# Steps of the woven attention blocks stand one by one on TensorE: in the middle of a weight piece, in front of its last chunk, and behind it

## The reference, cut to what matters

```python
# MLA, and in the same form the memory attention (without mask)
s = einsum('bhqd,bhkd->bhqk', q_nope, k_nope) + einsum('bhqr,bkr->bhqk', q_rope, k_rope)
p = softmax(where(mask, s * scale, -inf))
o = einsum('bhqk,bhkd->bhqd', p, v)
# NSA: three such attentions share one query, and their results are summed with gates
out = g[..., 0:1] * o_cmp + g[..., 1:2] * o_sel + g[..., 2:3] * o_win
```

## Time and profile before

| what | value |
|---|---|
| median of three runs | 2646.47 us (2645.66 to 2646.92) |
| the profiled execution, own time | 2647.24 us |
| its span | 2645.4 us |
| PE busy | 2614.7 us, 99% of the span |
| DVE busy | 1791.5 us, 68% |
| ACT busy | 1270.6 us, 48% |
| PE's share of the chain that ended last | 94% |

### The profile page before, as it was taken

One profiled execution on the slowest core, in us unless ns is written; L12 is line 12 of the kernel. 1 busy time (PEld: TensorE's weight loads), 2 busy tenths in 40 slices (PEclk: granted clock), 3 DMA queues, 4 the chain that ended last, 5 costly groups with the idle time before them and its releaser, 6 DMA issues.

```text
span 2645.4 us, 34673 instructions
## 1 busy us (share of the span) xinstructions
PE 2614.7 (99%) x14268; PEld 2256.2 (85%) x14268; DVE 1791.5 (68%) x2140; ACT 1270.6 (48%) x1689; POOL 13.1 (0%) x26
## 2 busy tenths in 40 slices
PE   8999999999999999999999999999999999999998
PEld 7898888888889888888888888888889898899987
DVE  7876897777666686676665545456676658766765
ACT  6546645443545444444443344445454545545554
POOL 0000000000000000000000000000000000000000
PEclk9999999999999999999999999999999999999999
DMA  9998817888685476477766555565656557654343
GB/s 351 363 359 266 271 44 264 313 286 286 223 274 140 129 270 238 143 277 251 246 215 235 192 191 191 190 203 179 191 171 200 181 184 238 210 180 142 97 160 127
DMA packets 339761, 573.53 MB, mean 217 GB/s; under 512 B 22671, under 2 KB 100807, under 8 KB 338328
## 3 DMA queue, kind: packets, MB, share of 16 engines
q1 hardware_dynamic: 336802, 560.45, 63.4%
q0 software_dynamic: 2368, 10.77, 1.2%
q10 hardware_dynamic: 438, 0.15, 0.0%
HBM read 567.11 MB, written 4.21 MB: 216 GB/s over the span
## 4 chain that ended last, share of the span: by engine, by line
PE 94%; DVE 2%; ACT 1%; DMA 1%; issue 1%; SPq 0%; ACTq 0%; DVEq 0%
PE tile_ps L1052 86%; PE misc_ps L1052 6%; DVE w_lo L2251 1%; DMA w_raw<-in_w_in 1%; PE misc_ps L1447 1%; PE misc_ps L1287 1%; DMA w_raw<-in_w_mem_kv 0%; ACT w_hi L1701 0%; DVE probs_t L2362 0%; PE misc_ps L1551 0%; PE misc_ps L1184 0%; ACT mem_t L1942 0%; DVE o_lo L2564 0%; DVE o_hi L2563 0%; DVE var L2561 0%
## 5 line engine op out<-in xcount | busy, mean ns | idle before, releaser
L2251 DVE TENSOR_TENSOR w_lo<-w_raw,w_hi 128x1024 fp32r<-128x1024 f32 x840 | 1012.5, 1223 | 650.9 <-ACT w_hi L1701 646.7
L1701 ACT ACTIVATE w_hi<-w_raw 128x1024 fp32r<-128x1024 f32 x840 | 878.4, 1058 | 1028.3 <-PE tile_ps L1052 958.1
L1052 PE MATMUL tile_ps<-w_hi,h_both 128*128 128x512 f32 x3008 | 818.3, 391 | 1.1 <-DVE h_both L2484 0.8
L1052 PEld LDWEIGHTS tile_ps<-w_hi,h_both 128*128 128x128 f32 x3008 | 561.4, 188 | 119.8 <-issue 5.2
L1052 PE MATMUL tile_ps<-h_both,w_hi 128*128 128x256 f32 (+1 forms) x2624 | 490.9, 312 | 2.1 <-DVE w_lo L2251 1.8
L1052 PE MATMUL tile_ps<-w_lo,h_both 128*128 128x512 f32 x1504 | 464.2, 389 | 0.0
L1052 PEld LDWEIGHTS tile_ps<-h_both,w_hi 128*128 128x128 f32 x2624 | 358.8, 192 | 3.6 <-DVE w_lo L2251 2.4
L1052 PEld LDWEIGHTS tile_ps<-w_lo,h_both 128*128 128x128 f32 x1504 | 282.3, 188 | 59.2
L1052 PE MATMUL tile_ps<-h_both,w_lo 128*128 128x256 f32 x1632 | 289.4, 281 | 0.0
L1052 PEld LDWEIGHTS tile_ps<-h_both,w_lo 128*128 128x128 f32 x1632 | 259.1, 191 | 28.4
L2342 DVE SCALAR_TENSOR_TENSOR probs_t<-w_raw,c_act,probs_t 128x512 f32<-128x512 f32 x210 | 157.7, 751 | 6.6 <-DMA w_raw<-in_ada_w 0.6
(11 more groups left out here) (408 smaller groups left out, 2126.1 us busy)
## 6 DMA issues: line engine op xcount, KB each, us to landing
w_raw<-in_w_in SPq DMA_DIRECT2D x88, 1024.0 KB, 5.2
w_raw<-in_ffn_w_in SPq DMA_DIRECT2D x88, 1024.0 KB, 5.1
w_raw<-in_ada_w SPq DMA_DIRECT2D x64, 1024.0 KB, 5.1
w_raw<-in_w_out SPq DMA_DIRECT2D x48, 1024.0 KB, 5.2
w_raw<-in_ffn_w_down SPq DMA_DIRECT2D x44, 1024.0 KB, 5.2
w_raw<-in_b_w_in SPq DMA_DIRECT2D x33, 1024.0 KB, 5.3
w_raw<-in_ada_w SPq DMA_DIRECT2D x64, 512.0 KB, 6.3
w_raw<-in_a_w_in SPq DMA_DIRECT2D x32, 1024.0 KB, 5.4
```

The lines of the kernel that those rows point to most:

```text
L1052: return nc.tensor.matmul(o, l, r, start=start, stop=stop, skip_group_check=True)
L1701: f(w_hi[CUT_IN.get(s_, s_ % 2)][:, hf], w_raw[r % 4][:, hf], ACT.Copy).then_inc(cut_hi, 1)
L2251: v.tensor_tensor(w_lo[b][:, hf], w_raw[r % 4][:, hf], f32(w_hi[b][:, hf]), ALU.subtract).then_inc(cut_lo, 1)
```

## The change

The last step of an entry stays behind its piece. The steps ahead of it are now called inside the piece: the first in front of its third chunk (number 2 of 0 to 3), that is after half of its matmuls, and of three steps the second in front of the fourth chunk. This is done by a new argument `inside` of `product`, a table from (piece, chunk) to a step. The arithmetic is the same, and so is the order of the steps among themselves. The program order of ACT, DVE, POOL and SP isn't changed at all: listed row by row, those of before and of the changed kernel are the same.

```diff
+        def spread(steps, sizes, piece=0):
+            inside, after, at_ = {}, [], 0
+            for e, n in enumerate(sizes):
+                for k in range(n - 1):
+                    inside[piece + e, 2 + k] = steps[at_ + k]
+                after.append(steps[at_ + n - 1])
+                at_ += n
+            return inside, after
...
-            def product(name, x_hi, x_lo=None, ready=(), chunk_ready=None, between=(), peel=False):
+            def product(name, x_hi, x_lo=None, ready=(), chunk_ready=None, between=(), peel=False, inside={}):
...
                         for c in range(0 if by_halves else g.kc):
                             k = q * g.kc + c
                             begin, end = k == 0, k == g.kp * g.kc - 1
+                            if (e_, c) in inside:
+                                inside[e_, c]()
                             if g.split and c == second:
                                 pe.wait_ge(cut_lo, low + per(i, 2 * g.body * g.kp))
...
-                product(f"mla_qn{hf}", *q_op, ready=done("cq"), between=drain[0:2])
-                product(f"mla_qr{hf}", *q_op, between=drain[2:3])
+                first, second = ({}, {}) if not drain else ({(0, 2): drain[0]}, {(0, 2): drain[3]})
+                product(f"mla_qn{hf}", *q_op, ready=done("cq"), between=drain[1:3], inside=first)
+                product(f"mla_qr{hf}", *q_op, between=drain[4:5], inside=second)
...
-            product("mla_wo", *o, chunk_ready=head_pairs, between=drain + woven[3:])
+            product("mla_wo", *o, chunk_ready=head_pairs, between=[drain[1], drain[2], drain[4]] + woven[3:],
+                    inside={(0, 2): drain[0], (2, 2): drain[3]})
...
+            mem_inside, mem_a = spread(mem_a[2:], MEM_A_GROUPS[1:])
...
+            steps, n = attention_steps("nsa"), [sum(sizes) for sizes in NSA_GROUPS]
+            inside, after = spread(steps[2:n[0]], NSA_GROUPS[0][1:], 5)
+            product("nsa_zq", *h, inside=inside, between=[None] * 4 + [lambda: (nsa_q_ready(), steps[0](), steps[1]())] + after)
+            inside, after = spread(steps[n[0]:], NSA_GROUPS[1])
+            product("nsa_qm", *h, inside=inside, between=after)
+            inside, after = spread(steps[n[0] + n[1]:], NSA_GROUPS[2])
+            product("nsa_zm", *h, inside=inside, between=after)
...
+            inside, after = spread(mem_b[1:], MEM_B_GROUPS[1:], 1)
+            product("nsa_out", *o, chunk_ready=heads_or_mem, inside=inside, between=[lambda: (steps[-1](), mem_b_ready())] + after)
```

More of the change, by code:

```diff
@@ L1495, in _ @@
                 pe.wait_ge(rp_done, ROPE0[f"mla_q{hf}"] + BLK)
-                drain = drained(attention_steps(f"mla{hf}", f"mla_v{hf}"))
+                steps = attention_steps(f"mla{hf}", f"mla_v{hf}")
+                for do in steps[:-5]:
+                    do()
+                drain = steps[-5:]
             fin = lambda a: [(at_fin, FIN0[a] + sum(u["last"] for u in UNITS[a]))]
@@ L1591, in mem_a_ready @@
                 pe.wait_ge(ld_mkv, 32)
-            mem_a = in_groups(attention_steps("mem_a"), MEM_A_GROUPS)
-            product("pool_zm", *h, between=placed({3: lambda: (mem_a_ready(), mem_a[0]())}))
+            mem_a = attention_steps("mem_a")
+            product("pool_zm", *h, between=placed({3: lambda: (mem_a_ready(), mem_a[0](), mem_a[1]())}))
+            mem_inside, mem_a = spread(mem_a[2:], MEM_A_GROUPS[1:])
             def pooled_or_mem(k):
@@ L1602, in _ @@
             product("pool_out", *o, chunk_ready=pooled_or_mem,
-                    between=placed({**{k: do for k, do in enumerate(mem_a[1:])},
+                    inside=mem_inside, between=placed({**{k: do for k, do in enumerate(mem_a)},
                                     **{k: lambda tb=tb: turn_residual("kv", tb) for tb, k in enumerate((9, 11, 14))}}))
@@ L1665, in heads_or_mem @@
                 return [(at_fin, FIN0["nsa"] + k + 2)] if k % 2 == 0 else []
-            product("nsa_out", *o, chunk_ready=heads_or_mem, between=with_mem_b(rest, [mem_b_ready] + mem_b[1:]))
+            inside, after = spread(mem_b[1:], MEM_B_GROUPS[1:], 1)
+            product("nsa_out", *o, chunk_ready=heads_or_mem, inside=inside, between=[lambda: (steps[-1](), mem_b_ready())] + after)
         @block.scalar
```

## The result

| what | before | changed |
|---|---|---|
| median | 2646.69 us (4 runs, 2645.66 to 2647.60) | 2680.32 us (4 runs, 2677.87 to 2683.39) |
| profiled execution | 2647.24 us | 2680.93 us |
| ratio | | 1.0126, 95% interval 1.0114 to 1.0138 |

The change costs 33.6 us, 1.3%. The forecast was 23.8 us and a range that ended at 2677 us: the direction was right, the size was not.

The account below looks back on a forecast made before the run. PE, busy for 99% of the span, bounds the kernel. New waits in NSA 15.9, MLA 5.9 and the last memory attention 2.0 sum to 23.8 us; added to 2646.5 us that gives 2670.3 us, range 2660 to 2677 us.

Parts of the forecast that it names:

- the stock of 5 us: PE's waits for DVE's o_lo (3.5 us) and ACT's transposes copy (1.4 us): about 5 us that spreading could gain.
- the spread gains what it is meant for: Rival: the old sum's write is ready in mid-piece, so only gains are left; 2641 us, chance 0.03.
- The mechanism and the formula: Inner steps whose values open a sum wait for its old write: 2.92 us moved up + 0.14 - slack.
- the sum took 2.0 us off: NSA: ACT starts the next cut 0.2 to 0.9 us sooner at five pieces; estimate 2.0 us, bounds 0 and 4.5.
- the sum has 2.25 us: NSA, the one inner step of `nsa_zq` that opens a sum: slack 0.81 us, so a wait of 2.25 us.
- NSA's 15.9 us: NSA: waits at nine inner steps, 18.9 us, less 1.0 for stalls and 2.0 for ACT's earlier starts.
- MLA's 5.9: MLA: four inner steps that open a sum lose 0.6, 0.8, 2.7 and 1.8 us, 5.9 us in all.
- the last memory attention's 2.0 us: Last memory attention: waits of 1.9 and 2.2 us, less gains of 1.1 and about 1.0 us; together +2.0 us.
- Broken runs at nothing: Breaking runs of weight matmuls at about 30 more places costs nothing; upper bound 0.1 us each, 3 us.
- the clock: Rival: PE's new idles in the attention blocks make the granted clock fall too, 1.7 us a fall; chance 0.10.
- this rival for a few falls: Clock falls behind the three to five new idles above 2.5 us: 5 to 9 us more, 2677 us; chance within 0.10.
- the case with all fifteen falls: Clock falls behind all fifteen new idles: 25 us more, 2696 us; chance 0.02 for nearly all, within the 0.10.

Follow-up runs that it names:

- early write: Changed kernel, but DVE writes each sum at the end of the entry before's last step, ahead of its next weight cut: 2642.28 us, ratio 0.9976.
- filled waits: Changed kernel with matmuls on constants, never read, in all 15 inner steps whose values waited 0.9 us or more for o_lo: 2670.89 us, ratio 1.0086.
- NSA alone: Kernel before the change, with the steps of NSA alone parted as in the change: 2669.57 us, ratio 1.0080.

## Why the prediction was right, and where it was wrong

**What bounds the kernel, and the stock of 5 us: right.** With the early write the spread gains 5.8 us. The stock read from the earlier trace rows was 4.9 us and small stalls; of the 4.9 us, 1.0 is still waited, so some 1.9 us of the gain are stalls too short to be listed as waits. The rival "the spread gains what it is meant for" named 2641 us and its condition, the write ready in the middle of the piece. The early write makes that condition true, and the time is 2642.28 us.

**The mechanism and the formula: right.** The new waits are at the 15 places, ten of them within 0.3 us of the forecast's numbers. One number in the sum was a slip: at the second place of the earlier trace rows the slack of 0.14 us gives 2.92 + 0.14 - 0.14 = 2.92 us, not 3.06; with the 0.39 us that PE waited there already it is 3.31 us. `nsa_qm` and `nsa_zm`, worked out from the earlier trace rows against measured: 2.92 + 0.39 against 3.28, 1.05 against 0.93 and 0.95, 1.94 against 1.85, 2.78 against 2.26, and 2.28 against 1.81 three times. MLA, worked out from the earlier trace rows: 1.6, 2.7, 1.8, 1.8 against 1.39, 2.51, 1.61, 1.71. The last memory attention: 2.2 and 1.9 against 2.12 and 1.59. Four places are half a microsecond shorter, 3 x 0.47 + 0.52 = 1.9 us, and for that the sum took 2.0 us off, for ACT's earlier start of the cut. The two rows of the changed kernel behind the first of these four show it: piece and cut start at

```profile
2478.09 0.72 PE L1062 MATMUL tile_ps<-h_both,w_hi 128*128 128x256 f32 x4
...
2479.19 1.99 ACT L1723 ACTIVATE w_hi<-w_raw 128x1024 fp32r<-128x1024 f32 x2
```

which is 1.10 us apart, where the earlier trace rows has 1.45 us: 0.35 of the 0.47 us. The forecast for PE's waits was over 20 in number and some 25 us; they are 18 and 27.6 us.

**One term was too large.** In `nsa_zq`, at the earlier trace rows's first place, the sum has 2.25 us and the trace 0.95. ACT's cut is why. Before, it began 1.64 us into the piece; these two rows of the kernel before are the start of the piece and the cut:

```profile
2428.83 0.72 PE L1052 MATMUL tile_ps<-h_both,w_hi 128*128 128x256 f32 x4
...
2430.47 1.99 ACT L1701 ACTIVATE w_hi<-w_raw 128x1024 fp32r<-128x1024 f32 x2
```

and these of the changed kernel:

```profile
2435.08 0.72 PE L1062 MATMUL tile_ps<-h_both,w_hi 128*128 128x256 f32 x4
...
2435.52 1.99 ACT L1723 ACTIVATE w_hi<-w_raw 128x1024 fp32r<-128x1024 f32 x2
...
2440.22 0.68 PE L1062 MATMUL misc_ps<-probs_t,v_cmp 15*128 15x128 f32 x4 [0.95 <-DVE o_lo L2586]
```

There it begins 0.44 us into the piece, 1.20 us sooner, because ACT had served the parted step already. The slack that I read from the old trace was itself a product of the grouping. This is the greater part of the 2.0 us by which NSA's 15.9 us differ from the 13.93 us with filled waits. MLA's 5.9 and the last memory attention's 2.0 us measure 5.73 and 2.27 us, and pooling 0.01 us.

**Broken runs at nothing: borne out, not measured.** The version with the early write has all of them and is 5.8 us faster than before; no run prices a break by itself.

**The step that failed: the clock.** The prediction says "by the rows, in which waits below a microsecond do nothing and only one of nearly 3 us did, I keep 2670", gives the rival 0.10, lets "idles above 2.5 us (three to five)" bring a fall, and puts the term at nothing in the sum. The trace of before didn't bear that out. Besides the fall of the earlier trace rows it has one at 154.16 us, which the prediction doesn't mention. In the 4.8 us ahead of it PE waited twice, for 1.18 and for 0.42 us (timeline), and in the last 3.41 us it was busy for 2.98 us (windows):

```profile
150.55 1.95 PE L1052 MATMUL misc_ps<-const,probs_t 128*128 128x1 f32 x16 [1.18 <-DVE probs_t L2362]
152.92 0.74 PE L1052 MATMUL tile_ps<-h_both,w_hi 128*128 128x256 f32 x4 [0.42 <-DVE w_lo L2251]
```

```profile
150.75:154.16 3.41, 2.98 (x26) 2.90 (x26) 2.48 (x4) 1.81 (x2) 0.00 (x0) 1.00 1.05 393
154.16:157.58 3.42, 3.42 (x18) 3.42 (x18) 0.81 (x2) 3.09 (x6) 0.00 (x0) 0.50 1.03 377
```

Behind a wait of 1.38 us at 160.43 the same trace has no fall. So I had put the border near 3 us, where a fall behind much shorter waits already stood against it, and left the whole term out of the sum.

In three profiles of the changed kernel the idles in the attention blocks of 2.12, 2.26 and 3.28 us were followed by a fall each time, that of 2.51 us in two of three, the four of 1.81 to 1.85 us in seven cases of twelve, and none of 1.71 us or less. In the first profile that is eight times 3.41 us at half clock and 12.5 us by the traces, the whole of what was missing: 23.8 us, less 1.9 for terms that were too large, plus 12.5 is 34.4 us, where the table has 34.5. The rule that the prediction weighed, from the Trainium skill, page "TensorE: Matmul & The Clock Gate", section "HAM oscillation — how this bites in real kernels", that PE begins cold after its wait in every turn, held for seven of fifteen waits in the first profile. The forecast of this rival for a few falls, 2677 us, lies 3 us below the median. The chance it was given was too low, and so was the upper end of the range, since the case with all fifteen falls (2696 us) was left outside.

What stays open: what decides whether a fall comes. Idles of 1.84 and 1.85 us in two other kernels, and one of 3.27 us early in a third, had none; the same idle in the same program had one in some executions and not in others. The profiles show that it is neither the program nor the length alone, and no more.

## What to carry to other kernels

Before a step is moved up on one engine, look at what its inputs stand behind in the program order of the others, and move both: here the spread alone cost 34 us, the write ahead of the cut alone gave nothing, and the two together gained 5.8 us (0.24%). When a change makes PE wait where it didn't, price each wait twice, as the wait and as the slower matmuls behind it: here the slower matmuls added 12.5 us to 22.0. Before a term is put at nothing, go through every place of the trace where the effect shows, not the clearest one alone: the trace of before had a fall behind waits of 1.18 and 0.42 us, and it was left out. Where a border isn't known, the range has to hold both sides.

## What the runs showed of the hardware that was not expected

The granted clock fell behind single idles of PE as short as 1.81 us, in a kernel in which PE is busy for 98% of the span, and once, in the trace of before, behind two waits of 1.18 and 0.42 us; yet it stayed at 1.00 behind an idle of 3.27 us in the kernel with NSA alone. A fall read 0.50 for 3.41 us, in a few cases for twice that (behind the 2.26 us wait in the first profile, behind the 3.28 us wait in the others), and cost 1.5 to 1.7 us per 3.41 us. Matmuls on constants in the idle time, whose result nobody reads, kept the clock at 1.00 and took 12.5 us off the loss in the traces (10.4 us by the medians), although they do no work. Where the falls stand differs from one execution of the same program to the next, with waits equal to 0.02 us, and their number (eight, five, eight) moved the time by 4.4 us between the traces.
